# Last two units of down weights split into free activation tiles, and the last square summed by TensorE

## The reference, cut to what matters

```python
def conv_ffn(h, w_gate, w_up, conv_w, w_down):
    a = causal_depthwise_conv(h @ w_gate, conv_w)
    return (jax.nn.gelu(a) * (h @ w_up)) @ w_down

x = x + gate2 * conv_ffn(h, w_gate, w_up, conv_w, w_down)   # FFN_DIM = 2816
return rms_norm(x, final_g)    # x * rsqrt(mean(x*x, channels) + EPS) * g
```

## Time and profile before

| | |
|---|---|
| median of three runs | 1966.34 us (1964.09 to 1970.80) |
| the profiled execution | 1966.72 us, span 1964.8 us |
| mean granted clock of TensorE | 0.985 |
| TensorE matmuls busy | 1881.5 us (96% of the span), x14012 |
| VectorE busy | 945.9 us (48%) |
| ScalarE busy | 472.4 us (24%) |
| GpSimd busy | 915.3 us (47%) |
| last down product of the loop ends | about 1894 us |
| gate and up product of the last tile | 1894 to 1916 us |
| last down product and final norm | 1922 us to the end |

### The profile page before, as it was taken

How to read it: one execution, slowest core, us unless ns; L and a number is a source line. 1 busy time by engine, 2 the same in 40 slices (tenths; PEclk the granted TensorE clock), 3 DMA queues, 4 the chain that set the end, 5 groups by cost and what they waited for, 6 DMA issues and landing times.

```text
span 1964.8 us, 33381 instructions
## 1 busy us (share of the span) xinstructions
PE 1881.5 (96%) x14012; PEld 1503.3 (77%) x14012; DVE 945.9 (48%) x1467; ACT 472.4 (24%) x734; POOL 915.3 (47%) x1100
## 2 busy tenths in 40 slices
PE   3999999999999999999999998999999999999995
PEld 1777777767787787787777786788888888888884
DVE  5883478754546546545434824532232323322325
ACT  4351344352212212212213314310110101101103
POOL 2676556523323223223224573464665655655645
PEclk7999999999999999999999999999999999999998
DMA  8561212232122122122125520111111111111112
GB/s 331 179 237 51 86 56 69 81 126 79 59 72 77 60 72 77 61 71 80 42 98 193 207 94 33 33 43 54 53 43 45 52 53 43 49 47 53 43 43 85
DMA packets 69686, 163.48 MB, mean 83 GB/s; under 512 B 5952, under 2 KB 30528, under 8 KB 69568
## 3 DMA queue, kind: packets, MB, share of 16 engines
q1 hardware_dynamic: 62080, 142.88, 21.6%
q10 hardware_dynamic: 7488, 18.88, 2.6%
HBM read 133.16 MB, written 28.57 MB: 82 GB/s over the span
## 4 chain that ended last, share of the span: by engine, by line
PE 45%; POOL 22%; issue 20%; DVE 8%; DMA 2%; ACT 2%; SPq 1%; POOLq 0%; ACTq 0%; DVEq 0%
PE gbank L585 30%; POOL w_hi L507 11%; POOL w_lo L511 10%; PE mbank L903 3%; DMA fa<-in_w_ada 2%; PE gbank L1050 1%; DVE state L2063 1%; DVE fa L1821 1%; PE gbank L903 1%; PE mbank L659 1%; PE mbank L826 1%; PE gbank L680 1%; DVE fa L1749 1%; PE mbank L1064 1%; DVE fa L2127 1%
## 5 line engine op out<-in xcount | busy, mean ns | idle before, releaser
L507 POOL TENSOR_TENSOR w_hi<-w_raw,zero 128x256 fp32r<-128x256 f32 (+1 forms) x520 | 397.6, 795 | 966.5 <-PE gbank L585 796.3
L585 PE MATMUL gbank<-h_hi,w_hi 128*128 128x512 f32 x1680 | 671.4, 400 | 5.4 <-ACT fa L1233 2.7
L585 PE MATMUL gbank<-h_lo,w_hi 128*128 128x512 f32 x1680 | 662.2, 394 | 0.0
L585 PE MATMUL gbank<-h_hi,w_lo 128*128 128x512 f32 x1680 | 660.3, 393 | 0.0
L511 POOL TENSOR_TENSOR w_lo<-w_raw,w_hi 128x256 fp32r<-128x256 f32 (+1 forms) x520 | 464.0, 923 | 10.2
L585 PEld LDWEIGHTS gbank<-h_hi,w_hi 128*128 128x128 f32 x1680 | 316.0, 188 | 84.6 <-issue 14.1
L585 PEld LDWEIGHTS gbank<-h_hi,w_lo 128*128 128x128 f32 x1680 | 315.7, 188 | 68.9 <-issue 2.0
L585 PEld LDWEIGHTS gbank<-h_lo,w_hi 128*128 128x128 f32 x1680 | 316.1, 188 | 67.0 <-issue 3.3
L1141 PE MATMUL mbank<-ra,w_hi 128*128 128x512 f32 x640 | 197.0, 389 | 0.0
L1141 PEld LDWEIGHTS mbank<-ra,w_hi 128*128 128x128 f32 x640 | 120.1, 188 | 25.0
L2221 DVE SCALAR_TENSOR_TENSOR fa<-mbank,mod,fa 128x1024 f32<-128x1024 f32 x40 | 51.4, 1284 | 169.2 <-PE mbank L1141 169.2
(11 more groups left out here) (339 smaller groups left out, 2169.1 us busy)
## 6 DMA issues: line engine op xcount, KB each, us to landing
w_raw<-in_w_tail SPq DMA_DIRECT2D x74, 512.0 KB, 3.5
fa<-in_w_ada SPq DMA_DIRECT2D x48, 512.0 KB, 6.3
w_raw<-in_w_in SPq DMA_DIRECT2D x26, 512.0 KB, 4.0
p_scr<-fa ACTq DMA_DIRECT2D x20, 512.0 KB, 2.6
w_raw<-in_w_mix SPq DMA_DIRECT2D x16, 640.0 KB, 4.0
fa<-in_xT SPq DMA_DIRECT2D x16, 512.0 KB, 7.7
w_raw<-in_w_gate SPq DMA_DIRECT2D x16, 512.0 KB, 3.9
sig_scr<-fa ACTq DMA_DIRECT2D x32, 256.0 KB, 2.0
```

The source lines that it names most:

```text
L507: last = pool.tensor_tensor(hi[:, c], raw[:, c], zero[:, 0:1].to_broadcast([P, w]), ALU.add)
L585: mm = pe.matmul(gb[bank], w, r, start=(q == 0), stop=(q == 3 * ks - 1))
```

## The change

Three things change, all at the end of the program.

1. GpSimd's loop over the feed-forward units ends one round earlier, and the last two units, 134 and 135, are split in code of their own. They go to `ra`: high parts to tiles 2 and 3, low parts to 6 and 7. Both wait for `half_done` 140, the end of the last group's down products (which are the last readers of these tiles), where before unit 134 waited for the gate product of the last tile (142) and unit 135 for its up product (144). `fin_down` reads its weights from there.
2. GpSimd adds 13 squares and no longer 14. The square of the last output tile in the second half is added by TensorE: `fin_sum(1, ...)` multiplies first the accumulator and then the slot of that square by ones, into one bank.
3. The first half's sum and root (TensorE and ScalarE) come after output tile 3 of the second half and not after 2, and VectorE begins with the norms of the first half one output tile later.

```diff
@@ GpSimd @@
-            with pool.Fori(0, (UNITS - U_FFN) // 2 - 2) as i:
+            with pool.Fori(0, (UNITS - U_FFN) // 2 - 3) as i:
                 for n in range(2):
                     split(i * 2 + (U_FFN + 4 + n), n, i * 16 + 16 * (U_FFN // 2 + 3),
                           used=(sem("half_done"), i * 4 + (2 * KT + 6 + 2 * n)))
 
-            for n in range(2 * (KT - 1)):
+            for n in range(2):
+                u = UNITS - 2 + n
+                split(u, n, 16 * (u // 2 + 1), used=(sem("half_done"), NG * 2 * UG + (2 * KT + 4)), to=(ra[:, 2 + n, :], ra[:, 6 + n, :]))
+
+            for n in range(2 * (KT - 1) - 1):
...
@@ TensorE @@
-                    w = (w_lo if which == 2 else w_hi)[:, m // 4, (m % 4 * 2 + k) * P:(m % 4 * 2 + k + 1) * P]
+                    w = ra[:, (6 if which == 2 else 2) + m // 4, (m % 4 * 2 + k) * P:(m % 4 * 2 + k + 1) * P]
...
             def fin_sum(hf, bank):
-                pe.wait_ge(sem("fin_acc"), (hf + 1) * (KT - 1))
-                pe.matmul(bank, m_("ones"), fa[:, ACC, hf * HALF:(hf + 1) * HALF], start=True,
-                          stop=True).then_inc(sem("sq_summed"), 1)
+                pe.wait_ge(sem("fin_acc"), KT - 1 if hf == 0 else 2 * (KT - 1) - 1)
+                mm = pe.matmul(bank, m_("ones"), fa[:, ACC, hf * HALF:(hf + 1) * HALF], start=True, stop=hf == 0)
+                if hf == 1:
+                    pe.wait_ge(sem("fin_sq"), 2 * KT)
+                    mm = pe.matmul(bank, m_("ones"), fin_sq_slot(2 * (KT - 1) - 1), start=False, stop=True)
+                mm.then_inc(sem("sq_summed"), 1)
...
-                if m == 2:
+                if m == 3:
                     pe.wait_ge(sem("fin_add"), KT)
                     fin_sum(0, fin_bank[KT - 1])
@@ ScalarE @@
-                    if hf == 1 and m == 2:
+                    if hf == 1 and m == 3:
                         fin_root(0, fin_bank[KT - 1])
@@ VectorE @@
-                if m >= 4:
-                    fin_norm(m - 4, 0)
-            for k in range(KT - 4, KT):
+                if m >= 5:
+                    fin_norm(m - 5, 0)
+            for k in range(KT - 5, KT):
                 fin_norm(k, 0)
```

## The result

The changed kernel took 1956.37 us in the median of nine runs (1951.88 to 1960.94) against 1966.82 for the kernel before (nine runs, 1964.09 to 1971.88): ratio 0.9946, 95% interval 0.9933 to 0.9958. The forecast was 1955.3, 11.2 us less than before; it is 10.45 less.

A forecast was written before the change was run, and what follows sets the result against it. TensorE was taken as busy nearly everywhere, then a pause, a slow clock and an end relay over engines. 6.31 + 2.89 + 2.1 - 0.1 = 11.2 us off 1966.72 gave 1955.5, forecast as 1955.3; range 1951.5 to 1960.

The forecast's parts named there:

- Steps 1 and 2: Last down product: both splits end 2.6 us early, the 6.31 us pause goes; last tile's low part 0.4 us early.
- Step 3: First 18 matmuls of the last down product: without a pause they run at full clock, giving back 2.89 us.
- Step 4: First sum over partitions, moved behind output tile 3: six matmuls (1.36 us) fit into a 2.08 us wait, costing nothing.
- Step 5: Last sum over partitions: the last square as an added TensorE product costs 0.53 us; root there at 1954.0 to 1954.6.
- Step 6: VectorE's norms at the end: VectorE, not the root, decides; second half starts 2.1 us earlier (bounds 0.6 and 2.8).
- Step 7: Stores at the end: 256 KB take 0.69 us against 0.65 to 0.67 of a norm, so 0.1 us is lost.
- The port: Tail: three norms each hold up GpSimd's last adds by a whole norm; second half gains only 0.6; 1957.0 us, chance 0.14.
- The wait: Last down product: unit 135's split comes 2.5 us too late, TensorE pauses again; 1960.9 us, no change, chance 0.05.
- The clock: Tail's 96 down matmuls: granted clock falls to 0.50 without a pause, 20.5 us more; 1974.8 us, slower, chance 0.03.

The follow-up runs named there:

- The fill of the pause: Kernel before, with 26 matmuls of overwritten result in TensorE's pause ahead of the last down product: ratio to before 0.9990, tail 47.6 us against 49.2.
- the splits alone: Kernel before, with only units 134 and 135 split into `ra`; 14 adds, first sum and norm order as before: ratio to before 0.9955, tail 40.4 us.
- With the clock held: Changed kernel with 10 matmuls of overwritten result ahead of the last sum over partitions: ratio to before 0.9949, tail 38.6 us against 39.5.

## Why the prediction was right, and where it was not

- **Steps 1 and 2, the splits fit and nothing else is late:** right. 2.5 us to spare (2.6 forecast), the low part 0.84 early (0.4 to 0.9). The fill of the pause and the splits alone show it from both sides.
- **Step 3, the clock comes back:** right, 9.19 us of pause and clock together. The fill of the pause shows the clock's part by itself: 2.7 us, 2.89 forecast.
- **Step 4, the first sum's place costs nothing:** right. 0.75 us of the gap is left where 0.72 was to be, and each later output tile is ready 1.4 us sooner.
- **Step 5, "An added fp32 product by the ones costs between 0.53 us [...] and 1.13 [...]. I take 0.53, since the first sum before it ran at clock 1.00 after a like wait":** this is the step that failed. The wait was like (2.42 us against 2.08), the clock was not: it fell to 0.50 within the sum, and the two products took 3.68 us. Even at the full clock the second costs 2.02 - 1.16 = 0.86 and not 0.53. The 0.53 was misread: it is the distance to the next matmul's start, and the matmuls behind it are held up further. The 24 behind the first sum take 6.04 us and the 24 ahead of it 5.60 (TensorE's timeline after), so that product costs 0.53 + 0.44 = 0.97; the rows of before have the same in two matmuls of 1.02 us right behind the sum, where other pairs take 0.61. The sum took 2.0 us longer than forecast (3.68 for 1.63): 0.4 by the product's cost, 1.7 by the clock. I had looked at the clock only where TensorE's wait was to go, and not where the change leaves a wait in front of more work than before.
- **Step 6, VectorE decides, 2.1 us:** wrong by the same cause. The root decided, and the tail's parts gave 0.57 us. With the clock held, the second half begins 41.26 - 30.24 = 11.02 us sooner, less 9.19: 1.8, with VectorE in an unbroken run, as step 6 had it. What is left of the 2.1 is 0.3 us. VectorE's first norm beside an add took 1.57 us where it took 1.30 before, which is as much; I take that for the cause, without a run that shows it.
- **Step 7, the stores lose 0.1:** in the change itself 0 (from the second half's first norm to the end 7.99 us, before 7.97), with the wait for the root gone 0.4. The size was off, and it was hidden.
- **The rivals.** The port eats 0.5 us of GpSimd's chain and not 2.2: an add waits for what is left of a norm, not for a whole one. The wait did not move. The clock did not fall under a full TensorE: it stood at 1.00 over all 96 down matmuls, from 1915.2 to 1939.

So 9.19 + 0.57 = 9.76 us of effect on the tail against 11.2 forecast. The measured difference of 10.45, with an interval from 8.3 to 13.2, can't tell the two apart, and that it lies only 0.75 from the forecast is in part chance: it does not bear out steps 5 and 6. The tails show the miss, within what their own executions allow. The last sum of before took 1.16 us in its profiled execution; with the pause filled, where that part is the same code, it took 2.12 and VectorE waited 1.01. Against a kernel before with such a sum the change would have gained about 9.7 + 1.0 = 10.7 us (an estimate). The splits carry the forecast; of the 2.0 us that steps 5 to 7 promised, 0.57 came in the profiled pair.

## What to carry to other kernels

TensorE's pause cost twice here, 6.3 us as itself and 2.7 to 2.9 in the clock behind it. The work to look at is what stands behind each wait that a change leaves or makes, not only behind the one that it removes. Work moved onto TensorE at the end of a wait is best priced at the slow clock: here 3.5 to 3.7 us, and 2.0 with the clock held. Buffers that fall free late in a program, such as activation tiles whose last reader is done, can take a conversion out of the last dependency for nothing; and once the end of a kernel is a relay over engines, its next bound, here a store of 256 KB every 0.69 us, may already lie 0.4 us behind the one removed.

## What I had not expected of the hardware

The granted clock fell at quite different distances from TensorE's last full work: in the kernel before about 5.2 us behind it (last down matmul done at 1950.1, clock 0.83 in the mean of 1954 to 1956), in the changed one 2.6 (done at about 1939.0, 0.91 in the mean of 1940 to 1942), in the filled kernel before about 2.0. So the 1.13 us of the last sum in the profile of before was a lucky one (1.42, 2.08 and 2.07 in the three other kernels with one product and a like wait), and one execution is not enough to price work behind a wait. It also rose again behind very little: in the changed kernel it stood at 0.97 to 1.00 from 1945 to 1948 (0.50 before and behind), when TensorE had done only the four fp32 matmuls of the last sum and then nothing.
